# Modulation groups 2 to 5 on four 32-column tiles of TensorE, 256 output columns each, in place of two 64-column tiles with 512

## The reference

```python
mod = (jax.nn.silu(c) @ w_mod[l] + b_mod[l])[:, None, :]          # and the same with c_ctx
shift1, scale1, gate1, shift2, scale2, gate2 = jnp.split(mod, 6, axis=-1)
mix, new_ctx = token_mixer(modulate(x, shift1, scale1), w_in, q_g, k_g, conv_w, conv_b, ..., ctx)
x = layer_norm(ALPHA * x + gate1 * mix, ln1_g, ln1_b)
ff = expert_choice_ffn(modulate(x, shift2, scale2), w_router, w_gate_up, w_down)
x = layer_norm(ALPHA * x + gate2 * ff, ln2_g, ln2_b)
```

## Time and profile before

| | us |
|---|---|
| median of 3 runs | 952.43 (951.62 to 954.9) |
| the profiled execution, its own time | 954.0 |
| its span in the trace | 952.2 |
| TensorE busy | 877.9 |
| VectorE busy | 772.6 |
| ScalarE busy | 573.8 |
| modulation matmuls (line 906), busy | 49.9 |
| TensorE idle just ahead of them | 14.3 |

### The profile page before, as it was taken

One profiled execution on the slowest core, in us unless ns is written; L12 is line 12 of the kernel. 1 busy time (PEld: TensorE's weight loads), 2 busy tenths in 40 slices (PEclk: granted clock), 3 DMA queues, 4 the chain that ended last, 5 costly groups with the idle time before them and its releaser, 6 DMA issues.

```text
span 952.2 us, 11590 instructions
## 1 busy us (share of the span) xinstructions
PE 877.9 (92%) x4615; PEld 599.9 (63%) x4615; DVE 772.6 (81%) x796; ACT 573.8 (60%) x586; POOL 158.8 (17%) x105
## 2 busy tenths in 40 slices
PE   2899999899999966899999999999999999999982
PEld 0389978356678843566666666666666666666651
DVE  2777636668779887789989989998998898898857
ACT  1335266735751333677777777777777777677732
POOL 1000300110011023103213303303311320320210
PEclk9999999989999987999999999999999999999996
DMA  8930500753048297999999999999999999999525
GB/s 281 396 121 1 205 1 1 294 127 112 2 166 325 107 351 285 347 419 388 415 389 390 416 382 387 401 394 381 389 406 380 375 410 373 381 396 394 194 58 190
DMA packets 57165, 272.08 MB, mean 286 GB/s; under 512 B 6772, under 2 KB 7016, under 8 KB 40728
## 3 DMA queue, kind: packets, MB, share of 16 engines
q1 hardware_dynamic: 48552, 243.81, 65.8%
q0 software_dynamic: 7120, 22.29, 8.5%
q10 hardware_dynamic: 1440, 5.24, 1.5%
HBM read 258.05 MB, written 13.28 MB: 285 GB/s over the span
## 4 chain that ended last, share of the span: by engine, by line
PE 84%; DVE 7%; DMA 4%; ACT 2%; issue 2%; SPq 0%; POOL 0%; DVEq 0%; ACTq 0%
PE PS L891 24%; PE PS L893 24%; PE PS L892 24%; DMA ring<-in_w_mod 3%; PE PS L1055 2%; PE PS L1039 1%; PE PS L1009 1%; PE PS L1078 1%; PE PS L906 1%; PE PS L1208 1%; PE PS L1197 1%; PE PS L1133 1%; DVE xf L1779 1%; DVE smin L1517 1%; ACT prob L700 1%
## 5 line engine op out<-in xcount | busy, mean ns | idle before, releaser
L1697 DVE TENSOR_TENSOR Wl<-wr,Wh 128x2048 fp32r<-128x2048 f32 x190 | 432.4, 2289 | 53.6 <-ACT Wh L811 53.5
L811 ACT ACTIVATE Wh<-wr 128x2048 fp32r<-128x2048 f32 x192 | 367.3, 1915 | 70.7 <-PE PS L893 70.6
L891 PE MATMUL PS<-Wh,Xh 128*80 128x512 f32 x512 | 203.0, 397 | 3.7 <-issue 2.9
L893 PE MATMUL PS<-Wl,Xh 128*80 128x512 f32 x512 | 201.8, 394 | 0.0
L892 PE MATMUL PS<-Wh,Xl 128*80 128x512 f32 x512 | 201.4, 393 | 0.0
L528 POOL DMA_INDIRECT acc_scratch<-ysc,idx_u x16 | 81.0, 5061 | 433.0 <-DVE ysc L1727 433.0
L891 PE MATMUL PS<-Wh,HTh 128*80 128x512 f32 x256 | 102.4, 400 | 3.1 <-DVE ysc L1727 3.1
L891 PEld LDWEIGHTS PS<-Wh,Xh 128*80 128x80 f32 x512 | 76.1, 149 | 43.9 <-issue 3.7
L893 PEld LDWEIGHTS PS<-Wl,Xh 128*80 128x80 f32 x512 | 76.0, 148 | 42.3 <-issue 0.4
L892 PEld LDWEIGHTS PS<-Wh,Xl 128*80 128x80 f32 x512 | 76.2, 149 | 39.7 <-issue 0.5
L892 PE MATMUL PS<-Wh,HTl 128*80 128x512 f32 x256 | 101.0, 395 | 0.0
(11 more groups left out here) (287 smaller groups left out, 1188.6 us busy)
## 6 DMA issues: line engine op xcount, KB each, us to landing
wr<-in_w_gate_up SPq DMA_DIRECT2D x128, 1024.0 KB, 9.8
wr<-in_w_down SPq DMA_DIRECT2D x64, 1024.0 KB, 8.9
ring<-in_w_mod SPq DMA_DIRECT2D x24, 1024.0 KB, 8.5
xt<-in_x_sample ACTq DMA_DIRECT2D x8, 512.0 KB, 8.1
ring<-in_w_in SPq DMA_DIRECT2D x4, 1024.0 KB, 12.7
ring<-in_w_out SPq DMA_DIRECT2D x4, 1024.0 KB, 11.1
w_qkv<-in_w_in SPq DMA_DIRECT2D x4, 768.0 KB, 11.9
h_scratch<-h POOLq DMA_DIRECT2D x5, 512.0 KB, 5.6
```

The source lines that it names most:

```text
L811: act.activation(Wh[n % NWH][:], wr[s][:], ACT.Copy).then_inc(W_hi, 1)
L891: pe.matmul(out, w[0], x[0], start=first, stop=False)
L893: return pe.matmul(out, w[0], x[1], start=False, stop=last)
L1697: dve.tensor_tensor(Wl[s][:], wr[s][:], Wh[n % NWH][:].bitcast(F32), ALU.subtract).then_inc(W_lo, 1)
```

## The change

In groups 2 to 5 each k now takes four matmuls: the stationary operand is `cT[:, k, 0:32]`, the moving operand a quarter of the row block (256 columns), and the output goes to 32 partitions and 256 columns of the bank. Groups 0 and 1 keep two matmuls of 512 columns. `c_ctx` moves from column 32 of `cT` to column 1, so that both vectors lie within the first 32 columns. The rows that count then stand in partitions 0 and 1 of each tile of 32 (or of 64, in groups 0 and 1). `b_row`, `m_row`, `b5_row` and `m5_row` are 256 columns wide instead of 512, `mod_row_sum` adds 128 x 256, and each DMA that stores or loads such a row moves four pieces of 1 KiB instead of two of 2 KiB. The number of these DMAs and the order of all instructions stay as they are; only the matmuls of line 906 go from 96 to 160.

```diff
-def halves(row):
-    return row.rearrange("a (h n) -> (a h) n", h=2)
+def quarters(row):
+    return row.rearrange("a (h n) -> (a h) n", h=4)
...
-    b_row, m_row = at("b_row", [P, H2], Dz + 3 * B10), at("m_row", [P, H2], Dz + 32768 + 3 * B10)
+    b_row, m_row = at("b_row", [P, D4], Dz + 3 * B10), at("m_row", [P, D4], Dz + 32768 + 3 * B10)
...
         def bias_row(m):
-            for row in (0, 32):
-                pool.dma_start(b_row[row:P:64, :], halves(t["b_mod"][:, (m + 2) * D:(m + 3) * D])).then_inc(brow_in, 16)
+            for row in range(2):
+                pool.dma_start(b_row[row:P:32, :], quarters(t["b_mod"][:, (m + 2) * D:(m + 3) * D])).then_inc(brow_in, 16)
 
         def store_row(m):
             pool.wait_ge(mod_row, m + 1)
-            for s, row in ((0, 0), (1, 32)):
-                pool.dma_start(halves(mods_dram[m, s:s + 1, :]), m_row[row:P:64, :]).then_inc(row_out, 16)
+            for s in range(2):
+                pool.dma_start(quarters(mods_dram[m, s:s + 1, :]), m_row[s:P:32, :]).then_inc(row_out, 16)
...
-        act.activation(cT[:, :, 32], cols[:, R_CTX:R_CTX + 8], ACT.Silu).then_inc(ct_ok, 1)
+        act.activation(cT[:, :, 1], cols[:, R_CTX:R_CTX + 8], ACT.Silu).then_inc(ct_ok, 1)
...
-                for half in range(2):
-                    last = pe.matmul(PS[MG * half:MG * half + MG, 512 * b:512 * b + 512], cT[:, k, :],
-                                     ring[:, k, 512 * half:512 * half + 512], start=(k == 0), stop=(k == KC - 1))
+                parts = 2 if g < 2 else 4
+                m, w = P // parts, D // parts
+                for part in range(parts):
+                    last = pe.matmul(PS[m * part:m * part + m, 512 * b:512 * b + w], cT[:, k, 0:m],
+                                     ring[:, k, w * part:w * part + w], start=(k == 0), stop=(k == KC - 1))
                 last.then_inc(mod_used, 1)
...
-            dve.scalar_tensor_tensor(out[:], PS[:, b:b + 512], 1.0 if m == 2 else 0.0, bias[:],
+            dve.scalar_tensor_tensor(out[:], PS[:, b:b + D4], 1.0 if m == 2 else 0.0, bias[:],
                                      ALU.add, ALU.add).then_inc(mod_row, 1)
```

More of the change, by code:

```diff
@@ L53 @@
 H2 = D // 2
+D4 = D // 4
 GRID_W = 64
@@ L235, in _build @@
     sh2 = [at("sh2s", [P, D], Fz + 32768), at("sh2p", [P, D], Fz + 36864)]
-    b5_row = at("b5_row", [P, H2], Fz + 36864)
-    m5_row = at("m5_row", [P, H2], Fz + 32768)
+    b5_row = at("b5_row", [P, D4], Fz + 36864)
+    m5_row = at("m5_row", [P, D4], Fz + 32768)
     wr = [at(f"wr{s}", [P, 2048], Dz + 8192 * s) for s in range(NSLOT)]
@@ L510, in _ @@
                 link(pool.memset(b5_row[:], 0.0))
-                for row in (0, 32):
-                    pool.dma_start(b5_row[row:P:64, :], halves(t["b_mod"][:, 5 * D:6 * D])).then_inc(brow_in, 16)
+                for row in range(2):
+                    pool.dma_start(b5_row[row:P:32, :], quarters(t["b_mod"][:, 5 * D:6 * D])).then_inc(brow_in, 16)
         def gather(e):
@@ L540, in _ @@
         pool.wait_ge(mod_row, 4)
-        for s, row in ((0, 0), (1, 32)):
-            pool.dma_start(halves(mods_dram[3, s:s + 1, :]), m5_row[row:P:64, :]).then_inc(row_out, 16)
+        for s in range(2):
+            pool.dma_start(quarters(mods_dram[3, s:s + 1, :]), m5_row[s:P:32, :]).then_inc(row_out, 16)
         pool.wait_ge(row_out, 128)
@@ L1312, in mod_cols @@
             for s_ in range(2):
-                last = dve.scalar_tensor_tensor(modT[:, w, s_, :].rearrange("p (h k) -> p h k", h=2), src[:, :, :, 32 * s_],
+                last = dve.scalar_tensor_tensor(modT[:, w, s_, :].rearrange("p (h k) -> p h k", h=2), src[:, :, :, s_],
                                                 plus, bias, ALU.add, ALU.add)
```

## The result

| | before | after |
|---|---|---|
| median | 953.78 (951.62 to 956.1, 20 runs) | 955.4 (954.7 to 959.44, 20 runs) |
| profiled execution, its own time | 954.0 | 956.27 |
| its span | 952.2 | 953.2 |
| TensorE busy | 877.9 | 871.7 |

The ratio is 1.0022, 95% interval 1.0014 to 1.003: the change costs about 2 us. The spans of the two profiled executions differ by 1.0 us and their own times by 2.3, because 3.1 us of the second lie outside its span, for 1.8 of the first. Forecast was 952.4 with "no change" as the likeliest; 955.4 is inside the range of 948.4 to 955.8, near its top.

A forecast was written before the change was run, and what follows sets the result against it. The prediction took the chain from gates to output projection as the bound, with group 4's two pieces on it. Its terms, -3.0 - 0.5 + 1.5 + 2.0 = 0.0, left the median of 952.4 us; range 948.4 to 955.8.

The forecast's parts named there:

- no change: Whole kernel: time stays within 2.9 us of the median before the change; chance 0.64.
- term 1: Group 4 on the chain: each of two pieces 1.5 us shorter on four tiles, -3.0 us.
- Term 2: mod_row_sum on the chain: 256 fewer columns save 0.27 us in each of two sums, -0.5 us.
- Term 3: Row DMAs, smaller pieces but the same number: taken as 0, with 0.5 us either way.
- term 4: Groups 2 and 3: their saving ends in the wait for the evacuation at 188.93, worth 0.
- term 5: Router's transposes and logits: longer idleness drops the clock to 1.2 GHz, +1.5 us, from 0 to +2.6.
- term 6: Start of the experts: group 5's shorter tail leaves them at 1.2 GHz, +2.0 us, from 0 to 3.7.
- slower: Whole kernel: slower by over 2.9 us; chance 0.14.
- the slow clock outlasts the start of attention: Attention units 1 and 2: up to 1.7 us longer, plus full router and expert losses, 956.9 at worst; chance 0.1.
- Lost at both: Router and start of experts: both lose the full clock, the forecast case, 950.5 to 954.5 us; chance 0.4.

The follow-up runs named there:

- e1: The changed kernel with group 5 back on two tiles: 951.34 us, ratio 0.9977 to the kernel before the change.
- e4: The changed kernel with every k of group 5 computed twice, first into an unread bank: 952.18 us, ratio 0.998 to the kernel before the change.
- e8: e1 with groups 0 and 1 on four tiles too: 952.87 us, ratio 0.9989 to the kernel before the change.
- e10: e7 with two more unused matmuls ahead of the router's last transposes: 949.07 us, ratio 0.9946 to the kernel before the change.
- e3: The changed kernel with four tiles in group 5 alone: 957.95 us, ratio 1.0037 to the kernel before the change.
- e9: The kernel before the change, all its tiles kept, plus four unused matmuls in TensorE's idle time: 953.18 us, ratio 0.9991.
- e2: The changed kernel with four tiles in group 4 alone: 951.72 us, ratio 0.9971 to the kernel before the change.
- e7: e1 plus eleven unused matmuls in TensorE's idle time around groups 2 and 3 and the attention loop's start: 949.26 us, ratio 0.9953.
- e6: The changed kernel with k = 0 to 4 of group 5 computed twice: 954.39 us, ratio 0.9998 to the kernel before the change.

## Why the forecast was wrong

The places were right, and so was the mechanism in the main: the clock takes back what group 4 gains. The sum came out at +1.0 in the profile and about +2 in the runs, instead of 0.0. Point by point:

- **Four tiles (term 1)**: right, and a little too small. 0.43 us per k, at the lower bound; by the chain a piece takes 1.86 us against the forecast 1.94. In the trace of after, in the first 0.07 us of a piece four records of line 909 are in flight, still four up to 210.20, and eight within 0.31 us:

```profile
209.97:210.04 0.07, 0.05 (x4) 0.05 (x7) 1.00 0.28 117
210.05:210.20 0.15, 0.15 (x4) 0.10 (x8) 1.00 0.78 300
209.99:210.30 0.31, 0.31 (x8) 0.22 (x12) 1.00 0.67 264
```

  A k of 8 records in 0.43 us, when one alone takes 0.214, needs four at a time. So the rule of the Trainium skill that spoke against it, strict program order ("TensorE: Matmul & The Clock Gate", "Part 3: Packing small matmuls"), does not bind here as the prediction applied it, with the two records of a matmul next to each other. The records don't name their tile, so whether the rule fails or the records stand in another order isn't shown. The 3.07 of the same section of the Trainium skill, for tiles in rows of the array, would give 0.56 us per k, an estimate; measured, 0.43. The loop gained 3.46 us for 3.0; twice 1.57 is in line 909 by the two chains (1.86 us a piece for 3.43), the other 0.3 in units 1 and 2. A piece in the chain of after:

```profile
204.06 1.86 PE PS L909 x32
```

  VectorE kept up:

```profile
206.66 0.82 DVE L575 COPY PT<-PS 128x640 f32<-128x640 f32 x1
212.00 0.42 DVE L1435 SCALAR_TENSOR_TENSOR m_row<-PS,b_row 128x256 f32<-128x256 f32 x1 [1.25 <-PE PS L909]
```

- **Narrow rows and their DMAs (terms 2 and 3)**: this step is the largest miss of the profile, +0.30 for -0.5. Term 2 was right: the sum went from 0.69 to 0.42 us, twice. Term 3 was not: the bias row's load was put at 0 with 0.5 either way, and it took 5.83 us in the chain of after for 4.93 in the earlier trace rows:

```profile
181.36 1.08 POOL mods_scratch L470 x2
182.98 5.83 DMA b_row<-in_b_mod
189.23 0.83 DVE PT L575
```

  The experiments show that most of this is scatter. In the chains of the eight kernels with narrow rows (after, e1, e4 to e8, e10) the load took 5.83, 5.21, 4.79, 5.33, 6.00, 5.41, 5.00 and 5.37 us, mean 5.37; in the three with wide rows where it is on the chain (before, e3, e9) 4.93, 5.18 and 5.22, mean 5.11. The fourth, e2, waits at this place for group 3 and its weights instead. The second transposes of unit 0 start, against 189.89, at +0.30, -0.09, -0.35, +0.18, +0.63, 0.00, -0.26 and +0.20 with narrow rows, mean +0.08, and at 0, +0.35 and +0.52 with wide ones, mean +0.29. So the narrow rows bring about 0.2 us where 0.5 was forecast, less than the scatter from one execution to the next; before's load was the shortest of its three and after's the second longest of its eight. A term of 0.5 us set against a wait for DMA needs more than one trace.
- **Groups 2 and 3 worth 0 (term 4)**: right in the medians, by e1 against e2. The saving went into 4.55 us of waiting for the evacuation, for 2.17 before.
- **The clock at the router (term 5)**: right in place and size, +1.53 for +1.5. All of it is in the logits; the transposes kept their 1.32 us, because the clock fell only behind them. Its reason, the length of the idle stretch, was too simple: e7 lost the clock after the same 1.38 us of idleness that did no harm before.
- **The clock at the experts (term 6)**: right in place, too small in size. 1.2 GHz lasted 4.8 us for the 3.3 assumed, and cost 2.19 + 0.30 us for 2.0. Its reason, a tail too short to bring the clock back, is not shown: in e6 the same short tail brought it back at 365.6, and it fell again at 369.0. The +0.22 ahead of it, between the logits and the experts' first transposes, is within what the experiments have at this place (-0.03 to +0.99).
- **What the sum stood on**: the median of 3 runs, 952.43, was 1.35 below the median of 20, 953.78. In that comparison the forecast of 0.0 missed by 1.6 us in medians, 2.1 by the ratio; the spans of the single profiles show 1.0. Over all executions with a span on record the median span is 953.4 for after (20) and 952.2 for before (75), 1.2 apart, so the profiles are not far off, and the rest lies between executions and outside the span. Within each kernel the executions with the longer spans tend to have the lower mean clock (correlation -0.61 over the 75 of before). That fits a clock that falls at other places in other executions, but one profile of each kernel can't show it.
- **The failing step** is thus the size of two terms, which had to be right to half a microsecond for a balance of 0.0. Term 3, the bias row's load put at 0, measured +0.9 in the profile (+0.3 in the means of the experiments). Term 6, the slow clock at the experts put at +2.0, measured +2.5. Term 1 brought 0.5 more than forecast (3.46 for 3.0) and made up for part of it. With both clock terms the loss was 4.0 us for the 3.5 forecast. Faster and slower were both near, and the chance of "slower", 0.14, was tied to a case in which the slow clock outlasts the start of attention. That case did not come: that stretch ended at 197.4 for 196.8 before. It was enough that the clock cost somewhat more at the two places named and that the bias row came later. "Lost at both" should have had its own share on the slower side.

## What to carry over

Before shortening TensorE work, ask what the work does for the clock of what stands behind it. Work in a gap that TensorE has to wait through anyway costs nothing here, and taking it out can cost more than a shortening on the critical path brings: here -2.8 us from group 4 (e2), +3.5 from group 5 (e3), with the same edit. Change only the groups on the critical path (e1, 0.9977), and try to fill TensorE's waits ahead of it with work that nobody reads (e7, 0.9953). And reckon terms under a microsecond against several traces, not one.

## What the runs showed of the hardware

- Four fp32 matmuls of 32 output partitions and 256 columns each run in 0.43 us as a set, twice as fast as the same product on two tiles (0.86 us), with no loss left for issuing eight records and eight weight loads.
- The 16 logits records of 16 columns each take 1.96 us at 2.4 GHz and 3.60 at 1.2 GHz, nearly double, though they are short. The transposes just ahead took 1.32 us in both kernels; the clock fell behind them.
- Eleven matmuls whose results nobody reads, 8.0 us in the trace of e7 (2.20, 1.56, 3.39 and 0.81), placed where TensorE waits, come with a faster kernel: e7 against e1, 0.0024 of the time, 2.3 us, give or take 2 by the two intervals.
